# A decoder layer on one core: both feed-forwards in two phases, with the hidden activations in DRAM between them and the output projections in seven products

## The reference, cut to what matters

```python
D_MODEL, SEQ, D_FF = 1024, 1024, 2816
def swiglu(x, w_in, w_out):            # w_in (1024, 5632), w_out (2816, 1024)
    g, u = jnp.split(x @ w_in, 2, axis=-1)
    return (jax.nn.silu(g) * u) @ w_out
u = modulate(rmsnorm(h, ffn1_norm[l]), sh1, sc1)
h = h + 0.5 * gt1[:, None, :] * swiglu(u, ffn1_w_in[l], ffn1_w_out[l])
u = modulate(rmsnorm(h, mix_norm[l]), sh2, sc2)
h = h + gt2[:, None, :] * token_mixer(u, ...)
u = modulate(rmsnorm(h, ffn2_norm[l]), sh3, sc3)
h = h + 0.5 * gt3[:, None, :] * swiglu(u, ffn2_w_in[l], ffn2_w_out[l])
return rmsnorm(h, final_norm)
```

## Time and profile before

| what | value |
|---|---|
| three timed runs | 2333.16, 2333.39, 2336.99 us, median 2333.39 |
| the profiled execution's own time | 2332.87 us |
| its span, first to last instruction | 2331.0 us |
| lies around the span | 1.87 us |
| PE busy | 2251.9 us, 97% |
| POOL, DVE, ACT busy | 1382.7, 1184.9, 533.6 us |
| mean granted TensorE clock | 0.987 |
| DMA over the span | 154.88 MB, mean 66 GB/s |

### The profile page before, as it was taken

One profiled execution on the slowest core, in us unless ns is written; L12 is line 12 of the kernel. 1 busy time (PEld: TensorE's weight loads), 2 busy tenths in 40 slices (PEclk: granted clock), 3 DMA queues, 4 the chain that ended last, 5 costly groups with the idle time before them and its releaser, 6 DMA issues.

```text
span 2331.0 us, 29992 instructions
## 1 busy us (share of the span) xinstructions
PE 2251.9 (97%) x10597; PEld 1823.2 (78%) x10597; DVE 1184.9 (51%) x2027; ACT 533.6 (23%) x1005; POOL 1382.7 (59%) x1280
## 2 busy tenths in 40 slices
PE   7999999999998999999998999999899999999997
PEld 4688888888887787777777788887788888888886
DVE  6646676665445417656656302243744444444445
ACT  5410000100113404455545201022411001101114
POOL 4797778878776533222112233335897777777774
PEclk9999999999999999999999999999999999999999
DMA  8113443442112210011101113111111111111111
GB/s 335 37 46 113 122 122 106 119 123 80 55 54 73 91 46 10 2 37 37 28 19 37 37 46 126 46 46 36 46 37 55 54 54 54 54 54 46 53 49 78
DMA packets 173209, 154.88 MB, mean 66 GB/s; under 512 B 5311, under 2 KB 149826, under 8 KB 172866
## 3 DMA queue, kind: packets, MB, share of 16 engines
q1 hardware_dynamic: 173122, 153.71, 21.4%
HBM read 145.30 MB, written 8.39 MB: 66 GB/s over the span
## 4 chain that ended last, share of the span: by engine, by line
PE 79%; DVE 8%; ACT 4%; issue 4%; POOL 2%; DMA 1%; SPq 1%; DVEq 0%; POOLq 0%; ACTq 0%
PE ps L2091 31%; PE ps L2141 20%; PE ps L2045 11%; PE ps L1962 11%; DVE h L1756 1%; DVE h L1779 1%; ACT h L1265 1%; DMA ada_full<-in_w_ada 1%; PE ps L2278 1%; PE ps L2007 1%; ACT rar L1129 1%; DVE rar L1632 1%; DVE nmx L1764 1%; PE ps L2353 1%; PE ps L2263 1%
## 5 line engine op out<-in xcount | busy, mean ns | idle before, releaser
L835 POOL TENSOR_TENSOR w_lo<-w_raw,w_hi 128x512 fp32r<-128x512 f32 x328 | 442.6, 1349 | 27.4
L2141 PE MATMUL ps<-hid,w_hi 128*128 128x512 f32 x1408 | 437.2, 392 | 6.4 <-DVE hid L1506 6.3
L2091 PE MATMUL ps<-t,w_hi 128*128 128x512 f32 x1280 | 394.2, 389 | 0.0
L833 POOL TENSOR_SCALAR w_hi<-w_raw 128x512 fp32r<-128x512 f32 x328 | 237.8, 725 | 211.6 <-PE ps L2141 117.7
L804 POOL TENSOR_SCALAR w_hi<-w_raw 128x1024 fp32r<-128x1024 f32 x57 | 60.8, 1067 | 501.7 <-PE ps L1962 312.5
L1574 DVE SCALAR_TENSOR_TENSOR h<-ps,gate_c,h 128x512 f32<-128x512 f32 x352 | 261.1, 748 | 155.6 <-PE ps L2141 155.0
L2141 PEld LDWEIGHTS ps<-hid,w_hi 128*128 128x128 f32 x1408 | 265.5, 189 | 64.0 <-issue 4.6
L2091 PEld LDWEIGHTS ps<-t,w_hi 128*128 128x128 f32 x1280 | 240.2, 188 | 50.2 <-POOL w_lo L835 0.4
L2141 PE MATMUL ps<-hid,w_lo 128*128 128x512 f32 x704 | 274.9, 390 | 0.0
L2091 PE MATMUL ps<-t,w_lo 128*128 128x512 f32 x640 | 249.0, 389 | 0.0
L2091 PE MATMUL ps<-b_low,w_hi 128*128 128x512 f32 x640 | 198.4, 391 | 1.3 <-DVE bufs L1560 1.3
(11 more groups left out here) (255 smaller groups left out, 3871.9 us busy)
## 6 DMA issues: line engine op xcount, KB each, us to landing
w_raw<-in_ffn_w_in SPq DMA_DIRECT2D x88, 512.0 KB, 3.8
ada_half<-in_w_ada SPq DMA_DIRECT2D x96, 256.0 KB, 2.7
w_raw<-in_ffn_w_out SPq DMA_DIRECT2D x44, 512.0 KB, 3.5
w_raw<-in_w_in SPq DMA_DIRECT2D x41, 512.0 KB, 3.6
ada_full<-in_w_ada SPq DMA_DIRECT2D x24, 512.0 KB, 11.1
x_tile<-in_x SPq DMA_DIRECT2D x8, 512.0 KB, 5.0
h_dram<-h SPq DMA_DIRECT2D x1, 4096.0 KB, 13.2
h<-h_dram SPq DMA_DIRECT2D x1, 4096.0 KB, 12.1
```

The source lines that it names most:

```text
L833: nc.gpsimd.tensor_scalar(hi, src, 1.0, 0.0, ALU.mult, ALU.add).then_inc(hs_high, 1)
L835: nc.gpsimd.tensor_tensor(lo, src, hi.bitcast(F32), ALU.subtract).then_inc(hs_ready, 1)
L2091: mm = nc.tensor.matmul(ps[bank][:], w[i], x[:, k, :], start=(first and k == 0 and q == 0), stop=(k == 3 and q == 2), skip_group_check=True)
L2141: mm = nc.tensor.matmul(ps[4 + i % 4][:], w[:, r // 2, c], x[:, j, half(hf)], start=(j == 0 and q == 0), stop=(j == 1 and q == 2))
```

## The change

The feed-forward gets two phases.

**Phase one**: `classic` tiles 0 and 1 and the 20 fast tiles back to back, no `down` between them. Odd and even tiles use different PSUM banks. DVE writes the finished hidden tile as plain float32 into `hid_raw` and forms, for each pair, four more half tiles from the four that it has (`hidden_sums`): seven operands, which SP writes to `hid_dram` (256 KB each, 77 for each feed-forward).

**Phase two** (`down`): the output projection over the whole depth in seven products of 11 steps. A step is one pair's operand with one 128x512 weight block: four output tiles by three matmuls, 12 matmuls. SP reads each operand back (`hidden_in`, four buffers `x_raw`), ACT makes the high part and DVE the low one (three buffers `x_op`). The whole of `w_out` is in SBUF in four quarters (`q00` to `q11`), loaded by six large DMAs when the last tile has freed the token operands; DVE (odd k) and POOL (even k) form the 44 weight sums between the steps of the first four products. DVE adds the banks to `h` after each product (`reads`, 28 additions).

**Who splits weights**: the high parts move from POOL to ACT (`high_hs`), POOL keeps the low ones (`low_hs`).

**At the ends**: the next norm's squares and sums are put between the last steps; its first `mean_square` stands after the last step; in `norm(1)` two squares and their sums are put behind the first two channel tiles. `first_units` and the first half tiles of `classic(0, 0)` go channel by channel over two units, and the 14 busy matmuls of `first_units` are gone. The loops are unrolled.

```diff
-            hid = at(st_, "hid", [P, 2, 2, S], F32R)
+            hid_raw = at(st_, "hid_raw", [P, 7, HALF])
+            x_op = at(st_, "x_op", [P, 3, 2, HALF], F32R)
+            x_raw = at(st_, "x_raw", [P, 4, HALF])
...
+            def down(f):                                   # SP
+                n = tile_hs(f, LAST)
+                sp.wait_ge(hs_used, n + 1)
+                sp.wait_ge(hid_out, 16 * (f * DOWN_STEPS + 7 * (PAIRS - 1)))
+                for i in range(4):
+                    hidden_in(f, i)
+                sp.wait_ge(hs_used, n + 2)
+                quarter_load(f, 0, q00[:, 2:10, :], 0, 0, 0, 8)
+                sp.wait_ge(hs_used, n + 3)
+                quarter_load(f, 1, q00[:, 0:2, :], 0, 0, 8, 10)
+                sp.wait_ge(hs_used, n + 5)
+                quarter_load(f, 3, q10[:], 1, 0, 0, PAIRS)
+                sp.wait_ge(hs_used, n + 7)
+                quarter_load(f, 2, q00[:, 10:11, :], 0, 0, 10, 11)
+                quarter_load(f, 4, q01[:], 0, 1, 0, PAIRS)
+                for i in range(4, 8):
+                    hidden_in(f, i)
+                hidden_out(f, LAST)
+                hidden_in(f, 8)
+                sp.wait_ge(hid_out, 16 * (f + 1) * DOWN_STEPS)
+                quarter_load(f, 5, q11[:], 1, 1, 0, PAIRS)
+                for i in range(9, DOWN_STEPS):
+                    hidden_in(f, i)
...
+            def down(f):                                   # POOL
+                for n in range(DOWN_STEPS):
+                    p, k = divmod(n, PAIRS)
+                    low_hs(down_hs(f, n), down_weight(n))
+                    if p < 4 and k % 2 == 0:
+                        weight_sum(nc.gpsimd, f, p, k)
+                    if 70 <= n:
+                        adds(2 * f + 1, n - 70, n - 69)
...
+            def down(f):                                   # ACT
+                for n in range(DOWN_STEPS):
+                    x_highs(f, n)
+                    if n + 3 < DOWN_STEPS:
+                        high_hs(down_hs(f, n + 3))
+                    if n >= 69:
+                        squares(2 * f + 1, n - 69, n - 68)
...
                 dve.wait_ge(tile_step, step(f, t, C01))
-                nc.vector.tensor_tensor(g1_b, g1_b, u2_b, ALU.mult).then_inc(tile_step, 1)
+                nc.vector.tensor_tensor(prod_place(t, 1), g1_b, u2_b, ALU.mult).then_inc(tile_step, 1)
+                hidden_sums(t, tile_step, step(f, t, PROD1))
+                piece_of()
+                piece_of()
...
+            def down(f):                                   # DVE
+                for n in range(DOWN_STEPS):
+                    p, k = divmod(n, PAIRS)
+                    dve.wait_ge(x_high, f * DOWN_STEPS + n + 1)
+                    nc.vector.tensor_tensor(x_op[:, n % 3, 1, :], x_raw[:, n % 4, :], x_op[:, n % 3, 0, :].bitcast(F32),
+                                            ALU.subtract).then_inc(x_ready, 1)
+                    if k == 1 and p > 0:
+                        reads(f, p - 1)
+                    if p < 4 and k % 2:
...
+                        weight_sum(nc.vector, f, p, k)
+                reads(f, 6)
...
+            def down(f):                                   # PE
+                for n in range(DOWN_STEPS):
...
+                    pe.wait_ge(hs_ready, down_hs(f, n) + 1)
+                    pe.wait_ge(x_ready, f * DOWN_STEPS + n + 1)
+                    w_h, w_l = hs_place(down_hs(f, n))
+                    for m in range(4):
+                        for q, (w, x) in enumerate(((w_h, 0), (w_h, 1), (w_l, 0))):
+                            mm = nc.tensor.matmul(ps[down_bank(p) + m][:], w[:, tile(m)], x_op[:, n % 3, x, :],
+                                                  start=(p in (0, 1, 3) and k == 0 and q == 0),
+                                                  stop=(k == PAIRS - 1 and q == 2), skip_group_check=True)
+                    mm.then_inc(hs_used, 1)
+                mean_square(2 * f + 1, 0)
```

More of the change, by code:

```diff
@@ new lines, in wa_count, with down_bank, bank_of, raw_halves @@
+        def wa_count(n):
+            return n // FFN_HS * (TILE_HS + DOWN_STEPS) + n % FFN_HS - 8 + 1
+        def down_bank(p):
+            return 0 if p % 2 else 4
+        def bank_of(t):
+            return 0 if t % 2 else 4
+        def raw_halves(t):
+            gate, up = 2 * t % SLOTS, (2 * t + 1) % SLOTS
+            return [w_raw[:, j, c * HALF:(c + 1) * HALF] for j in (gate, up) for c in range(2)]
+        def quarter(name, k):
+            if name == "Q00":
+                return q00[:, k + 2 if k < 8 else (k - 8 if k < 10 else k), :]
+            return {"Q10": q10, "Q01": q01, "Q11": q11}[name][:, k, :]
@@ L700, in ffn, with pieces @@
-                with sp.Fori(first, GROUPS - 1) as g:
-                    body(g)
-                body(GROUPS - 1, more=False)
+                for r in range(3, 7):
+                    columns_in(f, r)
+                def pieces(i0, i1):
+                    for i in range(i0, min(i1, 2 * KT * (N_MOD - 3))):
+                        ada_piece(3 + i // (2 * KT), i % (2 * KT))
+                if f == 0:
+                    sp.wait_ge(tlo_dve, 8)
+                    sp.wait_ge(tlo_pool, 8)
+                    pieces(0, 2)
@@ new lines, in ffn @@
+                for t in range(CLASSIC, FT):
+                    if t + 1 < FT:
+                        columns_in(f, 2 * t + 3)
+                    if t + 2 < FT:
+                        columns_in(f, 2 * t + 4)
+                    if t == CLASSIC:
+                        hidden_out(f, 0)
+                    hidden_out(f, t - 1)
+                    if f == 0:
+                        i0, i1 = pieces_in(t)
+                        pieces(i0 + 2, i1 + 2 if i1 else 0)
+                down(f)
@@ L1107, in fast_tile @@
-                act.wait_ge(hs_used, freed)
-                for hf, what in ((0, PROD0), (1, PROD1)):
-                    act.wait_ge(tile_step, step(f, t, what))
-                    high(f, t, jj, hf)
+                nc.scalar.activation(u2_b, ps[bank_of(t)][:], ACT.Copy).then_inc(p1_kept, 1)
+                high_hs(n + 6)
+                if t < LAST:
+                    high_hs(n + 7)
+                    high_hs(n + 8)
+                    high_hs(n + 9)
+                act.wait_ge(tile_step, step(f, t, C11))
@@ L1112, in ffn @@
             def ffn(f):
                 classic(f)
[L1116 to L1126 removed]
+                for t in range(CLASSIC, FT):
+                    fast_tile(f, t)
@@ new lines, in classic @@
+                        if (t, hf, i, k) == (0, 0, 0, 3) and n == 2:
+                            mean_square(n, 1)
+                        if f == 0 and t == 0 and i == 1 and k < 6:
+                            next(third_pieces)
+                        if f == 1 and (t, hf, i) == (0, 0, 0) and k < KT - 1:
+                            for _ in range(2):
+                                nc.tensor.matmul(ps[5][:], w_hi[:, 0, tile(k)], hi[:, k % 4, :], start=True, stop=True)
+                        if f == 0 and (t, hf, i, k) == (1, 0, 0, KT - 1):
@@ L2110, in fast_tile @@
                 if fresh:
                     sums_in(f, t, "T2")
-                product(n + 1, ring + 1, T2, 1, True)
+                product(n + 1, T2, b + 1, True)
+                if f == 0 and summed_in(t) is not None:
+                    pe.wait_ge(tile_step, step(f, t - 1, C10))
+                    column_sums(summed_in(t))
                 if fresh:
                     sums_in(f, t, "T3")
-                product(n + 2, ring + 2, T3, 3, True)
+                if f == 0 and (fresh or summed_in(t - 1) is not None):
+                    pe.wait_ge(mod_ready, 3 if fresh else summed_in(t - 1) + 1)
@@ L2116, in fast_tile @@
+                product(n + 2, T3, b + 3, True)
+                product(n + 3, T1, b + 2, True)
+                k = f * (FT - CLASSIC) + t - CLASSIC
+                pe.wait_ge(p1_kept, k + 1)
+                product(n + 4, B10, b, False)
                 if fresh:
                     sums_in(f, t, "T4")
-                else:
-                    pe.wait_ge(tile_step, step(f, t - 1, C01))
-                product(n + 3, ring + 3, T1, 2, True)
-                if sums is not None:
-                    sums()
```

691 lines of the change are left out of this document (322 added, 369 removed).

## The result

The changed kernel takes 2398.4 us (the median of four runs: three lie between 2397.2 and 2398.5, and the fourth, of 7736 us, is left out of the ratio), the kernel before beside it 2333.3 us. The ratio is 1.027, with a 95% interval of 1.026 to 1.029: **slower by 2.7%**, where 2306 us and a gain of 1.2% were forecast, and outside the range of 2287 to 2330. The profiled execution has a span of 2396.8 us, 65.8 more than before.

The account below looks back on a forecast made before the run. PE, busy 97% of the span, was taken as the bound. Matmuls saved 59.9 us, added waits and small savings left -27.2 in sum: 2332.9 - 27.2 = 2306 us (-1.2%); forecast 2297 to 2317, 58%, whole range 2287 to 2330.

Parts of the forecast that it names:

- In the tiles: Phase one's tiles: POOL and weight loads cause no wait; column sums late in feed-forward 1, +4 us (0 to 8).
- C: Rival, 7%: SP's queue moves quarters and operands at 138 GB/s; late loads cost 33 us per feed-forward, 2372 us.
- The matmuls: Output projections: 264 fewer matmuls at 0.2267 us each, -59.9 us, all on the path.
- What must keep up in phase two: Products 0 to 3: DVE and POOL need 29.2 us per 11 steps, under PE's 29.9; PE stays the bound.
- rival B: Rival, 20%: DVE and POOL operations never overlap in phase two's products 0 to 3; 2325 us, up to 2335.
- Start of phase two: PE waits 4.5 to 4.9 us for DVE's first low part, plus slow start; net +8.2 us.
- The boundaries: Between phase two's products: DVE's low part 1.0 us late at three boundaries per feed-forward, +6 us (0 to +10).
- the DMA: Phase two's loads of quarters and operands land in time or are hidden: 0 us, bound +4.
- Start of phase one's tiles: Before tile 2's third product PE waits on POOL, 4.2 and 6.0 us plus slow start; net +8.5 us.
- End of feed-forward 1: Next norm's mean square and root come after the last step, 7.5 us to PE's first matmul; +5 us (1 to 9).
- End of feed-forward 2: Four additions before the last scaling and a late second root; +4 us (2 to 7).

Follow-up runs that it names:

- the pieces left out: Changed kernel without the 96 half-row pieces of the modulation (SP loads and DVE operations; column sums add up other numbers): 2316.9 us.
- SP's order on top of the pairs: Changed kernel with DVE's pieces in pairs and SP asking for a tile's pieces behind the same pass's weight columns and hidden writes: 2326.8 us.
- SP's order: Changed kernel with only SP's piece loads shifted behind the weight columns of the next pass, DVE's places untouched: 2385.1 us.
- the pairs: Changed kernel with DVE's pieces two at a time, none behind the hidden sums of the tile that completes a chunk, SP's order untouched: 2359.7 us.
- the pairs on top of ACT's queue: Changed kernel with weight columns and hidden writes issued from ACT, and DVE's pieces in pairs: 2319.6 us, 0.994 of before.
- ACT's queue: Changed kernel with the tiles' weight columns and the hidden writes issued from ACT, only pieces left on SP's queue in the tiles: 2370.0 us.
- the writes alone: Changed kernel with the hidden writes alone issued from ACT, pieces and weight columns staying on SP in their order: 2411.3 us.

## Why the prediction was wrong

**The step that failed** is "In the tiles": "No wait", and "+4 (0 to 8)" for the column sums. It is worth 79 of the 93 us: with the pieces left out 82 us go, where the step had +4. I costed the edit there by DVE's seven operations, 7.4 us where PE comes after 5.4. I didn't cost what the edit does to SP. Three things were left out, and each can be read from the code and the earlier trace rows: the hidden writes (up to five of 256 KB per tile) are a new passenger on SP's queue, between the weight columns and the pieces; a piece's load waits for the use of the piece two before it, and with the last two pieces moved behind the hidden sums that use comes later (in tile 3 a piece is used at 159.6 and the next, behind three sums, at 168.8); and every weight load behind it waits along. How much each of the three costs isn't shown: SP's order on top of the pairs is worth 33 us, the pairs on top of ACT's queue 50, and the writes alone could not be priced. I took the load at 3.8 us from the earlier trace rows as if it were asked for when its slot is free. It lands 5.4 us after its issue now, and its issue is late:

```profile
w_raw<-in_ffn_w_in SPq DMA_DIRECT2D x88, 512.0 KB, 5.4
hid_dram<-hid_raw SPq DMA_DIRECT2D x154, 256.0 KB, 4.9
```

The rivals didn't hold it either. C looked at SP's queue, in phase two only, and for the rate of large loads, not for order.

**The matmuls**: right. Phase two of feed-forward 1 has 924 matmuls, 209.5 us at 0.2267, and takes 215.5 from its first to its last; 2.75 of the difference are waits, most of the rest is the first step at the low clock.

**What must keep up in phase two, and rival B**: right. From 640 to 660 DVE and POOL are both busy all the time, and so is PE:

```profile
640.00:660.00 20.00, 20.00 (x90) 16.57 (x89) 20.00 (x12) 8.08 (x14) 19.75 (x13) 1.00 0.37 106
```

By rival B, with the rule of the Trainium skill behind it ("SBUF — State Buffer", section "Who interferes with whom"), PE would have waited evenly through products 0 to 3, some 25 us in all. This trace doesn't agree with the rule for these operations: the pairs come every 1.70 us in this stretch, not 1.98, and all waits of PE at `x_op` are 15.7 us, in seven places.

**Start of phase two**: right. 4.57 and 5.17 of these 15.7 us (forecast 4.9 and 4.5).

**The boundaries and the DMA**: two errors that cancel. The boundaries, forecast at +6, cost 0.88 us, once: beside the four additions the low part was early enough at the others. The late operand behind `q11`, forecast at 0 with a bound of 4, costs 1.46 + 0.41 and, in feed-forward 2, 2.66 us; the seventh wait is 0.57 us, early in phase two of feed-forward 2. ACT and PE at that place of feed-forward 1:

```profile
624.19 0.63 ACT L1199 ACTIVATE x_op<-x_raw 128x512 fp32r<-128x512 f32 x1 [6.87 <-DMA x_raw<-hid_dram]
```
```profile
625.70 0.70 PE L2295 MATMUL ps<-x_op,w_hi 128*128 128x512 f32 x2 [1.46 <-DVE x_op L1752]
```

PE names DVE as the releaser; DVE had waited for ACT's copy, and ACT 6.87 us for the load of operand 9, which had stood behind a quarter as the prediction had it, only longer.

**Start of phase one's tiles**: waits of 5.0 and 4.1 us on POOL's low part (forecast 4.2 and 6.0), and a further one of 2.5 us in feed-forward 2 ahead of the second product, which I had not seen. The whole stretch of feed-forward 2 is 6 us dearer than forecast.

**End of feed-forward 1**: PE waits 7.53 us, forecast 7.5. To the next mark it is +8.5 and +2.9 ahead of it, 11 where +5 was forecast, the upper bound being 9. In the kernel without pieces the wait is 7.54 us and the stretch 890.8, so they are no follow-up of the stalls. The prediction had no term for the clock here: over the 50 us from the mixer's first matmul it averages 0.80, where it was 0.96 before, and PE waits 7.5 us in them in place of 3.8. The 14 busy matmuls are gone from that place too; how the 11 us divide among these wasn't tested.

**End of feed-forward 2**: 8.75 us of waiting for POOL's last sum of squares, +5.1 in all, forecast +4. (The prediction read 0.4 us from PE's end to the last scaling before; by 2311.25 - 3.31 = 2307.9 and 2308.66 in the earlier trace rows it is 0.7.)

The other terms together missed by 14 us on the dear side, though the boundaries came out cheaper: without the fault the change gives some 2317 to 2320 us (pieces left out; ACT's queue with pairs), a gain of 0.6 to 0.8% against the runs of before beside them, inside the range but little more than half of what was forecast.

## What to carry to other kernels

An in-order DMA queue is an engine of the sum: write down for one pass what stands in it, in order, what each entry waits for, and when it is reached, before and after. A load with a two-deep buffer may not stand in front of loads with slack. When a consumer is moved later, every entry behind its buffer's refill moves with it. If two faults stall the same place, mending one shows less than its worth: SP's order brought 13 us alone and 33 on top of the pairs, the pairs 39 alone and 50 on top of ACT's queue. Mend both before the form is judged.

## What the hardware showed unexpectedly

**Issuing isn't free when the queue is loaded.** A piece's load takes SP 0.33 us to issue, and so does a hidden write at best; five writes behind two weight loads took 5.11 us, and one took 3.7 (min, median, max in ns):

```profile
L732 SPq DMA_DIRECT2D hid_dram<-hid_raw x154: 319/580/3697, 130.7 to 2163.9; - x154
```

The two loads and five writes are 2.36 MB asked for in the 6.2 us from 171.98 on, or 380 GB/s, near the 393 of the earlier trace rows. In that stretch the DMA engines were 93% busy and moved 294 GB/s. SP seems to be held while they have too much in hand. That reading is argued from these rows and not tested.

**The clock behind a stall doesn't follow the stall's length, and it is worth less than it looks.** After 5.55 us of idle time the granted clock averaged 0.54 over the 10 us that followed, nearly all of it at 1.2 GHz. The sixteen thin matmuls of the column sums came first and took 3.55 us.

```profile
193.50:203.50 10.00, 9.97 (x33) 8.60 (x34) 1.34 (x3) 0.63 (x1) 6.00 (x5) 0.54 0.64 197
```

Behind the other five column sums it is 0.61 to 0.69, and the longest wait, 7.91 us, has 0.63. With ACT's queue a wait of only 2.69 us ahead of column sums has 0.66. But after 5.17 us of idle time ahead of phase two of feed-forward 2, whose matmuls are 128x512 from the start, it is 0.84, as good as the 0.83 after the 2.56 us of the earlier trace rows. So these rows part by what PE did first behind the wait and not by how long it waited. No run changed the one without the other.

Keeping PE busy in the waits held the clock up and gave back 3 of 15 us and 13 of 31. At the start of phase two the traces show why: the engine that was late sets the pace behind the stall, and the missing clock hides behind it. For the column sums this is argued only.
